# Expert weights taken in chunks of 1024 columns instead of 512, the last down product split by column half

## The chip, the cores and the metric

The kernel runs on one core of one Trainium2 chip. The metric is the device time of one execution in microseconds (us), as the median of several executions. The traces are of one profiled execution each.

## The reference

Two streams (256 prompt tokens and 64 sample tokens, 320 in all, width 1024) go through two layers. The second layer ends in a mixture of experts, which is what the change touches:

```
logits = (xf @ router).astype(jnp.float32)
top_v, top_i = lax.top_k(logits, TOP_K)                  # 2 of 8
gates = jax.nn.softmax(top_v, axis=-1)
for e in range(N_EXPERTS):
    y = y + combine[:, e:e + 1] * _swiglu(xf, w_gate[e], w_up[e], w_down[e])
# _swiglu: (silu(x @ w_gate) * (x @ w_up)) @ w_down, w_gate and w_up 1024 x 3584, w_down 3584 x 1024
x = layer_norm(ALPHA * x + y)
```

Everything is float32. All 8 experts' weights are read once (352 MB in the expert part).

## The kernel before

Every weight matrix comes in "units" of 1 MB (128 partitions x 2048 numbers). A unit passes four engines. SyncE issues its DMA into the ring `raw` (6 slots). ScalarE rounds it to the product format (`round_unit`, L993, writes `whi`). VectorE takes the remainder (`rest_unit`, L1250, writes `wlo = raw - whi`). TensorE multiplies with both: each float32 product is three products (hi*hi, hi*lo, lo*hi). `whi` and `wlo` are rings of 3 slots (SPLIT), so rounding unit n+3 waits until TensorE has used unit n, and both engines work two units ahead (AHEAD). Slots are in strict order: whatever stands between two units on ScalarE or VectorE delays the next unit.

Experts go in pairs, four pairs in this run: one `pair()` written out for the first, a loop for two, and one written out for the last (`FINAL`). For each pair 128 tokens per expert are gathered to `xg` (steps X, L877). A pair has 14 chunks of 512 columns (7 per expert), a chunk six units: gate (2 units, result in a PSUM bank), up (2 units, another bank), down (2 units, PSUM banks 4 and 5). The order is a list made by `pair_steps`: gate, T of the chunk before, gate, up, up, down of the chunk before twice. T turns the hidden rows: TensorE transposes `hm` (L931), ScalarE reads the bank into `hT_hi` (L1215), VectorE into `hT_lo` (L1764). After the second gate unit ScalarE makes `sg = silu(gate)` (L1191); after the second up unit VectorE makes `hm = sg * up` (L1738). Gate and up use banks 0 and 1 in even chunks, 2 and 3 in odd ones.

Small work hangs on VectorE behind `hm` of certain chunks: tables of the routing in the first pair (`tables`, chunks 0 to 7), the next pair's selection matrix (`make_pick`, L1672, chunk 9), and in the last pair the addresses of the tokens' rows (`rows_of_tokens`) and the sums of expert outputs into `acc` (`combine`, L1723: two each in chunks 6, 7 and 8, one in chunk 10, two in 11). In the last three chunks ScalarE and VectorE also split `acc` into `acc_hi` (L1197) and `acc_lo` (L1756). In the last chunk ScalarE loads the function table of the final norm (L1193).

Behind the last down product the residual `acc` is added through TensorE by an identity (`kept`, L951, L952), the last expert's output by the gate matrix (`newest`, L958 to L960), and VectorE normalizes three token tiles (L1788 to L1804).

Before the first pair, in `router()`, ScalarE and VectorE prepare x; the first two units are ready by then, the third is rounded only by `pair()`.

## Time and profile before

| | before |
|---|---|
| median of 3 executions | 1661.7 us (1661.43 to 1662.46) |
| the profiled execution | 1663.22 us, span of its instructions 1661.6 us |
| TensorE busy | 1630.2 us, 98% of the span |
| VectorE busy / ScalarE busy | 1228.0 us (74%) / 982.5 us (59%) |
| mean granted TensorE clock | 0.991 of full speed |
| expert part | from 638.64 us to the end |

The busy shares are over the whole span, of which the expert part is 62%. Idle time of an engine that is not the bottleneck costs nothing. The span and the execution's own time differ by 1.6 us, which no instruction of the trace fills.

### The profile page before, as it was taken

The page shows a single profiled execution, that of the slowest core. Times are in us where ns is not written, and L with a number is a line of the kernel's source. Part 1 is how long each engine was busy: PE and PEld are TensorE (multiplying, and loading weights), DVE is VectorE, ACT ScalarE, POOL GpSimd, SP SyncE. Part 2 cuts the span into 40 slices and gives each one's busy share as a digit, 9 for nine tenths or more (in the row PEclk, how much of TensorE's full clock was granted, in tenths as well). Part 3 has the DMA queues.
Part 4 walks back from the last instruction along what each step waited for, and adds up shares of the span by engine and source line. Part 5 has one row for each costly group of instructions (what it writes and reads, how often), then busy time and mean ns, then how long its engine had stood idle before and what let it go on. Part 6 is the DMA issues. An engine that isn't in the chain of part 4 may idle for free.

```text
span 1661.6 us, 22901 instructions
## 1 busy us (share of the span) xinstructions
PE 1630.2 (98%) x8756; PEld 1413.9 (85%) x8756; DVE 1228.0 (74%) x1050; ACT 982.5 (59%) x820; POOL 82.9 (5%) x91
## 2 busy tenths in 40 slices
PE   8999999999999999999999999999999999999996
PEld 7999999999989998787888888888888888777775
DVE  4567545445454766989887888887888888989987
ACT  4453433333344536777776777776777776776663
POOL 1001111111010000000000000000000000120200
PEclk8999999999999999999999999999999999999999
DMA  9424444444444243999998999998999999999992
GB/s 297 133 97 134 152 151 146 145 145 146 150 153 153 77 134 132 354 365 362 373 376 314 363 371 364 378 363 321 369 375 368 365 364 349 354 382 377 372 352 77
DMA packets 226500, 446.58 MB, mean 269 GB/s; under 512 B 10514, under 2 KB 72640, under 8 KB 226368
## 3 DMA queue, kind: packets, MB, share of 16 engines
q1 hardware_dynamic: 223856, 434.13, 73.5%
q0 software_dynamic: 2560, 11.29, 1.8%
q8 instruction: 58, 0.95, 0.2%
q14 instruction: 26, 0.21, 0.0%
HBM read 439.87 MB, written 8.67 MB: 270 GB/s over the span
## 4 chain that ended last, share of the span: by engine, by line
PE 88%; DVE 6%; ACT 2%; issue 2%; DMA 1%; SPq 1%; DVEq 0%; ACTq 0%
PE ps L918 15%; PE ps L901 12%; PE ps L903 12%; PE ps L902 12%; PE ps L590 10%; PE ps L592 10%; PE ps L591 10%; DVE wlo L1250 2%; ACT whi L993 2%; PE ps L877 1%; PE ps L931 1%; DMA raw<-in_moe_w_up 1%; PE ps L663 1%; PE ps L622 1%; DVE xl L1285 1%
## 5 line engine op out<-in xcount | busy, mean ns | idle before, releaser
L1250 DVE TENSOR_TENSOR wlo<-raw,whi 128x2048 fp32r<-128x2048 f32 x410 | 934.5, 2291 | 255.3 <-ACT whi L993 252.6
L993 ACT ACTIVATE whi<-raw 128x2048 fp32r<-128x2048 f32 x410 | 784.5, 1915 | 244.5 <-PE ps L592 85.1
L901 PE MATMUL ps<-whi,xg 128*128 128x512 f32 x896 | 360.9, 403 | 10.5 <-DVE wlo L1250 10.2
L903 PE MATMUL ps<-whi,xg 128*128 128x512 f32 x896 | 355.1, 396 | 0.0
L902 PE MATMUL ps<-wlo,xg 128*128 128x512 f32 x896 | 354.8, 396 | 0.0
L590 PE MATMUL ps<-xh,whi 128*128 128x320 f32 x832 | 259.8, 312 | 0.3
L591 PE MATMUL ps<-xl,whi 128*128 128x320 f32 x832 | 256.9, 309 | 0.0
L592 PE MATMUL ps<-xh,wlo 128*128 128x320 f32 x832 | 256.8, 309 | 0.0
L901 PEld LDWEIGHTS ps<-whi,xg 128*128 128x128 f32 x896 | 169.3, 189 | 55.4 <-DVE wlo L1250 15.5
L903 PEld LDWEIGHTS ps<-whi,xg 128*128 128x128 f32 x896 | 169.2, 189 | 40.1
L902 PEld LDWEIGHTS ps<-wlo,xg 128*128 128x128 f32 x896 | 169.4, 189 | 36.9
L590 PEld LDWEIGHTS ps<-xh,whi 128*128 128x128 f32 x832 | 156.5, 188 | 5.2 <-DVE xl L1285 2.4
L591 PEld LDWEIGHTS ps<-xl,whi 128*128 128x128 f32 x832 | 156.5, 188 | 0.2
L592 PEld LDWEIGHTS ps<-xh,wlo 128*128 128x128 f32 x832 | 156.4, 188 | 0.0
L918 PE MATMUL ps<-whi,hT_hi 128*128 128x512 f32 x448 | 140.8, 395 | 1.3 <-DVE wlo L1250 0.7
L918 PE MATMUL ps<-whi,hT_lo 128*128 128x512 f32 x448 | 141.0, 396 | 0.0
L918 PE MATMUL ps<-wlo,hT_hi 128*128 128x512 f32 x448 | 140.5, 394 | 0.0
L918 PEld LDWEIGHTS ps<-whi,hT_hi 128*128 128x128 f32 x448 | 83.9, 188 | 21.8 <-DVE wlo L1250 2.1
L918 PEld LDWEIGHTS ps<-whi,hT_lo 128*128 128x128 f32 x448 | 84.3, 188 | 19.9
L918 PEld LDWEIGHTS ps<-wlo,hT_hi 128*128 128x128 f32 x448 | 84.2, 188 | 19.9
L1215 ACT ACTIVATE hT_hi<-ps 128x512 fp32r<-128x512 f32 x56 | 33.6, 600 | 75.1 <-PE ps L931 74.8
L590 PE MATMUL ps<-hh,whi 128*128 128x320 f32 x224 | 69.0, 308 | 0.0
(287 smaller groups left out, 1378.8 us busy)
## 6 DMA issues: line engine op xcount, KB each, us to landing
raw<-in_moe_w_gate SPq DMA_DIRECT2D x112, 1024.0 KB, 7.4
raw<-in_moe_w_up SPq DMA_DIRECT2D x112, 1024.0 KB, 7.4
raw<-in_moe_w_down SPq DMA_DIRECT2D x112, 1024.0 KB, 6.9
raw<-in_w_in SPq DMA_DIRECT2D x24, 1024.0 KB, 5.5
raw<-in_ffn_w_gate SPq DMA_DIRECT2D x14, 1024.0 KB, 5.0
raw<-in_ffn_w_up SPq DMA_DIRECT2D x14, 1024.0 KB, 5.0
raw<-in_ffn_w_down SPq DMA_DIRECT2D x14, 1024.0 KB, 5.0
raw<-in_w_out SPq DMA_DIRECT2D x8, 1024.0 KB, 5.2
```

The lines of the kernel that those rows point to most:

```text
L590: pe.matmul(out, wh, hi, start=start and j == 0, stop=False)
L591: pe.matmul(out, wh, lo, start=False, stop=False)
L592: mm = pe.matmul(out, wl, hi, start=False, stop=stop and j == len(pairs) - 1)
L622: pe.matmul(bank[:, 0:P], mean_d[:], mean_d[:], start=True, stop=True)
L663: pe.matmul(ps[5][:, 0:T], mean_d[:], sq[:, k % 4, :], start=k == 0, stop=k == KT - 1).then_inc(var_part, 1)
L901: pe.matmul(bank[:], xh_k, wh, start=k == 0, stop=False)
L902: pe.matmul(bank[:], xh_k, wl, start=False, stop=False)
L903: mm = pe.matmul(bank[:], xl_k, wh, start=False, stop=k == KT - 1)
L918: mm = pe.matmul(ps[4 + d][:], hT[:, c % 2, k, :], slot(w, n, SPLIT, 2)[:, j, 512 * d:512 * d + 512], start=fc == 0 and k == 0 and hT is h ...
L993: act.activation(flat(whi, n, SPLIT), flat(raw, n, RAW), ACT.Copy).then_inc(hi_ready, 1)
L1215: act.activation(hT_hi[:, c % 2, :, :].rearrange("p f s -> p (f s)"), bank[:], ACT.Copy).then_inc(hT_hi_ready, 1)
L1250: dve.tensor_tensor(flat(wlo, n, SPLIT), flat(raw, n, RAW), flat(whi, n, SPLIT).bitcast(F32), ALU.subtract).then_inc(lo_ready, 1)
```

## The change

A chunk of a pair is now 1024 columns ("wide", number s, seven of them), except the middle one (s = 3, MID), which holds the last 512 columns of the first expert and the first 512 of the second. A gate or up unit of a wide chunk is 256 rows by 1024 columns (rows of 4 KB in memory instead of 2 KB), so gate fills banks 0 and 1, up banks 2 and 3, and there is no second set of banks. The number of units, products, transposes and bytes stays. Down units were rows of 4 KB already. A chunk is 4 gate units, T twice, 4 up units, 4 down units of the chunk before. Work that hung on chunk number c hangs on group g = 2s + q // 2 at up units with q = 1 or 3.

```diff
+        for s in range(WIDE):
+            steps += [("gate", s, q) for q in range(4)]
+            if s:
+                steps += [("T", s - 1, 0), ("T", s - 1, 1)]
+            if last and s == MID:
                 steps.append(("GT", 0, 0))
...
+            up = [("up", s, q) for q in range(4)]
+            down = [("down", s - 1, q) for q in range(4)] if s else []
+            if s == MID + 1:
+                steps += up[:2] + down[:2] + up[2:] + down[2:]
+            elif last and s == WIDE - 1:
+                steps += up + down[:2] + [("T", s, 0)] + down[2:] + [("T", s, 1)]
+            else:
+                steps += up + down
...
         if not last:
...
+            steps += [("X", 0, 0), ("X", 1, 0), ("T", WIDE - 1, 0), ("T", WIDE - 1, 1), ("X", 2, 0), ("X", 3, 0)]
+        return steps + [("down", WIDE - 1, q) for q in range(4)]
```

On ScalarE both silus stand behind the fourth gate unit, and the rounding of the third unit is moved from the start of `pair()` into `router()`, ahead of its reads of x (VectorE the same):

```diff
+                round_unit(U_MOE + AHEAD)
                 for n, j in enumerate(XT_ORDER):
...
-                        if part == "gate" and half:
+                        if part == "gate" and q == 3:
                             act.wait_ge(unit_used, upto(n + 1, i, PER_PAIR))
...
+                            if c:
+                                act.wait_ge(m_hid, upto(2 * c, i, PC))
+                            for b in range(2):
+                                act.activation(sg[:, b, :], ps[b][:], ACT.Silu).then_inc(m_silu, 1)
...
+                            if last and c == WIDE - 1:
                                 act.preload_act_table_set(LOG_EXP)
```

On VectorE:

```diff
-                        if part == "up" and half:
+                        if part == "up" and q == 3:
                             dve.wait_ge(unit_used, upto(n + 1, i, PER_PAIR))
...
+                            for b in range(2):
+                                dve.wait_ge(m_silu, upto(2 * c + b + 1, i, PC))
+                                dve.tensor_tensor(hm[:, b, :], sg[:, b, :], ps[2 + b][:], ALU.mult).then_inc(m_hid, 1)
+                        if part == "up" and q % 2:
+                            g = 2 * c + q // 2
                             if first:
...
+                                tables(g, step)
```

The last two down units of the last pair are multiplied together, first all for column half 0, then the residual of token tile 2, then all for half 1; the residuals of tiles 0 and 1 stand ahead of the last down product, and `combine` goes by column half:

```diff
+            def last_down(i, n):
...
+                pe.wait_ge(lo_ready, upto(n + 2, i, PER_PAIR))
+                for d in range(2):
+                    if d:
+                        kept(2)
+                    for q in (2, 3):
+                        for j in range(2):
+                            for hT, ws in ((hT_hi, (whi, wlo)), (hT_lo, (whi,))):
+                                for w in ws:
+                                    mm = pe.matmul(ps[4 + d][:], hT[:, 2 * q + j, :],
+                                                   slot(w, n + q - 2, SPLIT, 2)[:, j, 512 * d:512 * d + 512],
+                                                   start=False, stop=q == 3 and j == 1 and hT is hT_lo)
+                    mm.then_inc(ys_done, 1)
...
+            def combine():
...
+                for d, cols in enumerate(HALVES):
+                    pe.wait_ge(ys_lo_ready, d + 1)
+                    for t in range(TT):
```

VectorE's norm takes the statistics of column half 0 of all three tiles first, then goes tile by tile as before.

Where this moves instructions, in the order in which they stand on the engine. First ScalarE in the last chunk of the last pair, before, from the T ahead of the last gate unit:

```order
L1215 ACTIVATE hT_hi<-ps 128x512 [waits job_done]
L992 REGISTER_ALU [waits raw_landed3]
L993 ACTIVATE whi<-raw 128x2048 [waits unit_used]
L1189 REGISTER_ALU
L1190 REGISTER_ALU [waits unit_used]
L1191 ACTIVATE sg<-ps 128x512 [waits m_hid]
L1193 ACT_TABLE_LOAD
L993 ACTIVATE whi<-raw 128x2048 [waits unit_used,raw_landed4]
```

And ScalarE at the same place after the change (in the other wide chunks the rows are the same without the table load):

```order
L1030 ACTIVATE whi<-raw 128x2048 [waits unit_used]
L1227 REGISTER_ALU
L1229 REGISTER_ALU [waits unit_used]
L1231 ACTIVATE sg<-ps 128x512 [waits m_hid]
L1231 ACTIVATE sg<-ps 128x512
L1233 ACT_TABLE_LOAD
L1254 REGISTER_ALU
L1256 ACTIVATE hT_hi<-ps 128x512 [waits job_done]
L1254 REGISTER_ALU
L1256 ACTIVATE hT_hi<-ps 128x512 [waits job_done]
L1030 ACTIVATE whi<-raw 128x2048 [waits unit_used,raw_landed4]
```

Between two roundings stood one small operation at a time (one read of T, or one silu); now all four stand together. VectorE in the last pair, before, at chunk 7:

```order
L1250 TENSOR_TENSOR wlo<-raw,whi 128x2048 [waits hi_ready]
L1737 REGISTER_ALU [waits unit_used]
L1738 TENSOR_TENSOR hm<-sg,ps 128x512 [waits m_silu]
L1723 SCALAR_TENSOR_TENSOR acc<-y,gate_at,acc 128x1024 [waits y_fetched0]
L1723 SCALAR_TENSOR_TENSOR acc<-y,gate_at,acc 128x1024 [waits combined,y_fetched1]
L1249 REGISTER_ALU
L1250 TENSOR_TENSOR wlo<-raw,whi 128x2048 [waits hi_ready]
```

VectorE after the change, at groups 6 and 7 (s = 3):

```order
L1291 TENSOR_TENSOR wlo<-raw,whi 128x2048 [waits hi_ready]
L1765 SCALAR_TENSOR_TENSOR acc<-y,gate_at,acc 128x1024 [waits y_fetched0]
L1765 SCALAR_TENSOR_TENSOR acc<-y,gate_at,acc 128x1024 [waits combined,y_fetched1]
L1290 REGISTER_ALU
L1291 TENSOR_TENSOR wlo<-raw,whi 128x2048 [waits hi_ready]
L1290 REGISTER_ALU
L1291 TENSOR_TENSOR wlo<-raw,whi 128x2048 [waits hi_ready]
L1780 REGISTER_ALU [waits unit_used]
L1781 TENSOR_TENSOR hm<-sg,ps 128x512 [waits m_silu]
L1780 REGISTER_ALU
L1781 TENSOR_TENSOR hm<-sg,ps 128x512 [waits m_silu]
L1765 SCALAR_TENSOR_TENSOR acc<-y,gate_at,acc 128x1024 [waits y_fetched0]
```

The group at q = 1 has lost its `hm` product, the group at q = 3 has two of them ahead of its extra work.

## Rows read from the trace of the kernel before

**Rows 1.** The page's DMA issues: count, KB each, median us to landing.

```profile
raw<-in_moe_w_gate SPq DMA_DIRECT2D x112, 1024.0 KB, 7.4
raw<-in_moe_w_down SPq DMA_DIRECT2D x112, 1024.0 KB, 6.9
```

**Rows 2.** Waits, 640 to 1600 us: who waited for whom, us, times, longest.

```profile
ACT whi L993 <- DMA raw<-in_moe_w_gate: 5.1, 3, 2.8
PEld ps L901 <- issue: 3.0, 6, 0.7
```

**Rows 3.** The chain that ended last, inside the third pair: start us, us, what.

```profile
1163.81 5.58 PE ps L918 x24
...
1172.18 0.44 PE ps L931 x4
...
1180.98 5.57 PE ps L918 x24
```

**Rows 4.** Timeline in the second pair, around a silu: start us, us, engine, line.

```profile
909.82 0.40 PE L901 MATMUL ps<-whi,xg 128*128 128x512 f32 x1
...
910.02 0.60 ACT L1191 ACTIVATE sg<-ps 128x512 f32<-128x512 f32 x1 [0.39 <-PE ps L903]
...
910.52 1.91 ACT L993 ACTIVATE whi<-raw 128x2048 fp32r<-128x2048 f32 x1
...
912.46 4.61 DVE L1250 TENSOR_TENSOR wlo<-raw,whi 128x2048 fp32r<-128x2048 f32 x2 [0.51 <-ACT whi L993]
```

**Rows 5.** Timeline, the first product of the first expert pair.

```profile
638.64 0.39 PE L901 MATMUL ps<-whi,xg 128*128 128x512 f32 x1
```

**Rows 6.** The chain that ended last, first pair, around its third unit.

```profile
642.53 1.82 ACT whi L993
...
646.72 0.50 PE ps L901
...
648.05 0.43 PE ps L902
```

**Rows 7.** Windows: busy us (count) of each engine, PEclk, DMA share, GB/s.

```profile
647.80:651.00 3.20, 3.20 (x9) 2.51 (x8) 3.20 (x2) 0.61 (x1) 0.00 (x0) 0.50 0.89 308
...
1600.00:1603.40 3.40, 3.40 (x10) 2.52 (x10) 3.14 (x2) 0.00 (x0) 0.00 (x0) 0.51 0.95 327
```

**Rows 8.** Timeline in the router: both engines' idle time before.

```profile
622.98 0.56 DVE L1570 COPY lg<-ps 128x8 f32<-128x8 f32 x3 [5.25 <-PE ps L839]
...
623.96 0.60 ACT L1158 ACTIVATE xt_hi<-ps 128x512 fp32r<-128x512 f32 x1 [5.66 <-PE ps L848]
```

**Rows 9.** Timeline of VectorE, last pair, chunks 6 and 7.

```profile
1501.32 0.68 DVE L1738 TENSOR_TENSOR hm<-sg,ps 128x512 f32<-128x512 f32 x1
1501.91 2.67 DVE L1723 SCALAR_TENSOR_TENSOR acc<-y,gate_at,acc 128x1024 f32<-128x1024 f32 x2
...
1504.50 6.69 DVE L1250 TENSOR_TENSOR wlo<-raw,whi 128x2048 fp32r<-128x2048 f32 x3
...
1520.12 0.68 DVE L1738 TENSOR_TENSOR hm<-sg,ps 128x512 f32<-128x512 f32 x1
```

**Rows 10.** Timeline of VectorE, second pair, chunk 9.

```profile
1055.45 0.95 DVE L1672 TENSOR_TENSOR pick<-slot_no,q_tab 128x768 fp32r<-128x768 f32 x1
```

**Rows 11.** Timeline of TensorE, last pair, behind chunk 11.

```profile
1598.79 0.51 PE L901 MATMUL ps<-whi,xg 128*128 128x512 f32 x1 [2.29 <-DVE wlo L1250]
```

**Rows 12.** Timeline of the end.

```profile
1624.70 1.28 ACT L1193 ACT_TABLE_LOAD   x1
...
1630.29 0.73 PE L918 MATMUL ps<-whi,hT_hi 128*128 128x512 f32 x2 [0.74 <-DVE wlo L1250]
...
1637.11 0.73 PE L918 MATMUL ps<-whi,hT_hi 128*128 128x512 f32 x2 [0.54 <-DVE hT_lo L1764]
...
1642.79 0.39 PE L951 MATMUL ps<-acc_hi,ident_r 128*128 128x512 f32 x1
...
1645.55 1.31 DVE L1788 BATCH_NORM_STATS2 stats<-ps 128x6 f32<-128x512 f32 x2 [0.65 <-PE ps L960]
```

More of the change, by code:

```diff
@@ L883, in pair @@
                 unit, job = 0, GATHERS
-                for part, c, half in steps:
-                    a, fc = c // FC, c % FC
-                    if first and (part, c, half) == ("gate", 1, 0):
-                        pe.wait_ge(acc_ready, 2 * TT)
+                for part, c, q in steps:
+                    a = expert_of(c, q)
                     if part in ("gate", "up"):
@@ L1728, in pair @@
                 unit, job, turns = 0, GATHERS, 0
-                for part, c, half in steps:
+                for part, c, q in steps:
                     if part in ("gate", "up", "down"):
```

229 lines of the change are left out of this document (116 added, 113 removed).

## The prediction

> **What bounds the kernel now.** I read the page first, for the busy shares and the DMA issues, then the waits of the expert part, then the chain that ended last, then the timeline around each place that the change touches. TensorE is 98% busy, and in the expert part it is the bound in a plain sense: in the third pair one chunk takes 17.17 us from down product to down product, of which the 24 products of down are 5.57, a T is 0.44, and the 48 products of gate and up are the 11.16 left [rows 3]. So a product takes 0.232 us, whether its weights came in rows of 2 KB (gate, up) or of 4 KB (down), and a unit of 12 takes 2.79. There is no idle time in such a chunk to win. DMA is no bound: a 2 KB-row unit lands 7.4 us after its issue and a 4 KB-row unit 6.9 [rows 1], and the longest wait of a rounding for a gate transfer is 2.8 us, three waits and 5.1 us in all [rows 2].
>
> TensorE waits elsewhere. At the start of the experts the third unit is late: the first product starts at 638.64 [rows 5], two units later it is 644.22, the third unit starts at 646.72 because ScalarE rounds it only at 642.53 [rows 6]. And in the first and last pair VectorE's small work makes units late. These waits and the end are where the change can act.
>
> **The margin behind each unit.** Take as zero the moment at which a unit's next product starts. ScalarE's silu starts at +0.20 (910.02 against 909.82), the rounding behind it 0.50 later, VectorE's remainder 1.95 after the start of the rounding [rows 4]. A remainder takes 2.29 alone. TensorE continues about 0.17 after its end (from the case below). So before, +0.20 +0.50 +1.95 +2.29 +0.17 = 5.1, against 5.58 for the two units in hand: 0.47 to spare. On VectorE the same: at chunk 6 of the last pair hm starts at 1501.32, the sums follow at 1501.91, the next remainder only at 1504.50, and the next hm is 18.80 later than this one instead of 17.17 [rows 9]. So 0.59 for hm and 2.59 of extra work x cost 1.63: stall = x + 0.6 for each hm product - 1.56.
>
> **Part by part.**
>
> *Third unit rounded in the router: -4.1.* It removes the wait of 2.5 us (644.22 to 646.72). Behind it products stood at 0.43 instead of 0.23 [rows 6], the granted clock being 0.50, that is 1.2 GHz in place of 2.4 [rows 7]; eight such products lost 1.6. The cover in the router: ScalarE was idle for 5.66 us and VectorE for 5.25 [rows 8]; rounding 1.9 and remainder 2.3 in line are 4.2, so they fit with some 0.4 to 1 to spare; without that cover up to 4.2 would stand in front of the reads of x. The fourth unit is now the one rounded at 642.53; 642.53 + 1.95 + 2.29 + 0.17 = 646.94, and it is wanted at 647.01. What is late next: nothing.
>
> *Silus and T reads together: +2.3.* Behind the fourth gate unit ScalarE now has two silus and two reads of T before the next rounding: 0.20 + 4 x 0.50 + 1.95 + 2.29 + 0.17 = 6.6. TensorE has two T's and two units: 0.88 + 5.58 = 6.46. The wait is 0.1 to 0.15 each, in six chunks of four pairs, of which the last is taken below: 23 x 0.1 = 2.3. The margin is thinner than what I can read, so between 0 and 0.25 each: 0 to 5.8. Queued behind ScalarE's silus are only these roundings, and VectorE's remainder and TensorE wait for them in turn. With no T in the way (s = 0) two silus need 5.6 against 5.58: nothing.
>
> *Two hm products together: nothing in a plain chunk* (1.2 - 1.56 < 0), but in a group with extra work the even ones gain 0.6 and the odd ones lose 0.6, each cut off at zero. First pair, tables: before, six waits and 3.0 in all [rows 2], of which 2.2 show in the distances of the chunks. Groups 1, 5, 7 lose 0.6 each, groups 2 and 6 give back 0.15 and 0.6, group 3 (0.4) and the selection matrix in group 9 (0.65) begin to show: **+2.1**. Second and third pair: the matrix is 0.95 [rows 10], 0.87 to the next start; it was hidden (0.87 + 0.6 < 1.56), now 0.87 + 1.2 - 1.56 = 0.5 twice: **+1.0**. Last pair: groups 6 and 8 gain 0.6 each, group 7 loses 0.6 (1.6 to 2.2), group 11 loses 0.6 (TensorE's idle of 2.29 [rows 11], counted by distance 2.56, becomes 3.2), groups 0, 2 and 10 gain 0.1, 0.4 and 0.2, groups 1 and 3 lose 0.6 and 0.1: **0**.
>
> *Gathers: +0.5.* T twice between X1 and X2 lets X2 wait for the bank of the first T: 0.2 more, three times (an estimate; the T operations' 0.6 and 0.7 on ScalarE and VectorE follow each other, TensorE's T is 0.44).
>
> *The end: +3.6.* (a) The table load of 1.28 [rows 12] stood between one silu and a rounding and made the first down product of chunk 12 late by 0.9 (idle 0.74 [rows 12]). Now it stands in the row of four operations that has no margin: 0.1 + 1.3 = 1.5 at least. (b) In the last chunk hm twice and a split of acc (1.13 from start to start) give 0.77, less T's 0.44, plus 0.35 since (a) leaves VectorE later: 0.7; before 0.15. (c) `last_down` wants both last units at once. The last one reuses the slot of down unit 80 (counted in the pair), so its rounding starts only when 80 is used: 0.20 + 1.95 + 2.29 + 0.17 = 4.6 after it, while TensorE has just unit 81 in hand (2.79): 1.8. Before, the last but one product waited 0.8 for hT_lo (idle 0.54 [rows 12]), which goes. (a) to (c): 4.0 against 1.85, +2.1. (d) Twelve residual products of 0.2275, 2.7 us, stood behind the last down product at 1642.79 and now stand ahead of its end, where nothing idles long enough to hide them; in return the statistics begin 1.5 after that end (second column half to ys_lo 0.8, then 0.6) instead of 2.8 (1645.55). VectorE's tail is as long as before. +2.7 - 1.3 = +1.4.
>
> *4 KB rows: 0.* The transfers hide behind 11 us of units in the ring; of the waits in rows 2 at most 1.2 reached TensorE. The Trainium skill (DMA: Bandwidth & Descriptors, Where 436 GB/s comes from) puts the limit of a core's loads from HBM at about 358 GB/s, whatever the rows. By that rule longer rows would bring nothing either; the trace does not agree with the figure, since a unit of 1.049 MB in 2.79 us is 376 GB/s.
>
> **Sum**: -4.1 + 2.3 + 2.1 + 1.0 + 0 + 0.5 + 3.6 = +5.4. The profiled execution took 1663.2 and would take 1668.6; the median of the runs shown is 1.5 below it, so 1661.7 + 5.4 = **1667.1**.
>
> **Rivals.**
> - *The clock falls again.* Idle times of 2.5 and 2.6 us were followed by 3.4 us at 1.2 GHz [rows 7], those of 1.6 were not. The 2.2 of group 7 and the 1.5 and 1.8 of the end lie between. Each fall costs 1.6: one or two give 1668.7 to 1670.3. Chance 0.20. The Trainium skill (TensorE: Matmul & The Clock Gate, What's actually happening) says that activity releases the throttle and lack of it brings it back; the trace agrees.
> - *ScalarE's queue has just enough margin.* With no wait behind the silus 1667.1 - 2.3, and with the gathers' 0.5 hidden too 1664.3, within what counts as no change. Against it stands only a difference of 0.1. Chance 0.20.
> - *The product itself gets faster* (the other side). 4 KB rows might ease what slows a product; 2% off the 2688 gate and up products is 12.5 us, 1654.6. It decides from 8.7 us, 3.2 ns a product. For it: products step by 0.2275 at the very end, with no weights arriving. Against it: down products, with 4 KB rows, take the same 0.232 as gate and up [rows 3]. Chance 0.12.
> - *The silu wait is 0.25 or more* and adds up with late transfers: 1670 to 1672. Chance 0.06. The forecast itself has the 0.42 left.
>
> **How the numbers follow.** 0.2% (3.3 us) is what a measurement of this kernel can tell from no change. Faster: the third rival, 0.12. Same, up to 1665.0: the second rival and a lower part of the forecast, 0.24. Slower: 0.64. The range takes in the clock above and part of the faster case below: 1659.0 to 1671.5; the forecast's own is 1664.5 to 1670.
>
> **What would show it.** In the changed kernel the third unit should start 5.58 after the first, with the granted clock at 1.0. A chunk of the middle pairs should take 34.4 to 34.5 instead of 2 x 17.17 = 34.34; the chain should name ScalarE's hT_hi and a rounding at the first up unit. Group 9 should show 0.5 of idle, group 11 some 3.2 with slow products behind it. In the end, 1.8 of idle ahead of `last_down` on the remainder of the last unit, and statistics 1.5 behind the last product. A middle chunk under 34.2 would make me wrong as a whole; so would a product step under 0.230.

## The result: 1678.1 us against 1662.0, slower by 1.0%

The changed kernel takes 1678.08 us (median of 4 runs, 1677.68 to 1681.39) against 1661.99 for the kernel before beside it (4 runs, 1661.43 to 1662.46). The ratio is 1.0103, 95% interval 1.0088 to 1.0118. The prediction had 1667.1 and a range up to 1671.5: the direction was right, the loss of 16.1 us three times the 5.4 predicted. The profiled execution is the slowest of its four, 1681.39 us.

The loss by stretch, from the profiled spans of 1661.6 and 1679.8. The experts start at the same time (638.6). Between first gate loads the three pairs take 253.64, 251.49 and 249.79 us, where they took 253.84, 248.26 and 247.38; the last pair up to the end of TensorE's last product takes 273.1 instead of 261.8, and the tail behind that 13.1 instead of 11.8. So of the 18.2 us between the spans 11.4 are in the last pair.

The page of the changed kernel, DMA packets and DMA issues:

```profile
DMA packets 177347, 446.57 MB, mean 266 GB/s; under 512 B 10514, under 2 KB 72640, under 8 KB 177216
...
raw<-in_moe_w_gate SPq DMA_DIRECT2D x112, 1024.0 KB, 7.0
raw<-in_moe_w_up SPq DMA_DIRECT2D x112, 1024.0 KB, 7.3
raw<-in_moe_w_down SPq DMA_DIRECT2D x112, 1024.0 KB, 7.3
```

A gate unit now lands in 7.0 us instead of 7.4 [rows 1], a down unit, whose rows have not changed, in 7.3 instead of 6.9. The longer rows bought no time on the path.

**The start.** Timeline of the router in the changed kernel, then the first pair around the third unit:

```profile
618.80 1.89 ACT L1030 ACTIVATE whi<-raw 128x2048 fp32r<-128x2048 f32 x1
620.79 2.29 DVE L1291 TENSOR_TENSOR wlo<-raw,whi 128x2048 fp32r<-128x2048 f32 x1 [2.46 <-ACT whi L1030]
623.00 0.55 DVE L1612 COPY lg<-ps 128x8 f32<-128x8 f32 x3
623.81 0.60 ACT L1196 ACTIVATE xt_hi<-ps 128x512 fp32r<-128x512 f32 x1 [3.12 <-PE ps L862]
...
638.67 0.39 PE L921 MATMUL ps<-whi,xg 128*128 128x512 f32 x1
...
644.25 0.40 PE L921 MATMUL ps<-whi,xg 128*128 128x512 f32 x1
644.48 0.39 PE L922 MATMUL ps<-wlo,xg 128*128 128x512 f32 x1
```

Rounding and remainder fit into the idle time of [rows 8] (the copy of lg starts at 623.00 instead of 622.98), and the third unit starts at 644.25, 5.58 behind the first, where TensorE waited until 646.72 [rows 6].

**The last pair.** Who waited for whom on TensorE's weight loads, 1390 to 1640 us, in the changed kernel:

```profile
PEld ps L921 <- DVE wlo L1291: 9.7, 10, 2.7
PEld ps L947 <- DVE wlo L1291: 9.5, 9, 3.7
PEld ps L965 <- DVE hT_lo L1808: 1.8, 1, 1.8
```

The rows add up to 21 us, where the kernel before had 14.4 (L901 12.3 and L918 2.1). Almost all is VectorE's remainder being late, but not always because of VectorE. The longest wait of the first row, 2.66, goes back over a rounding to a weight transfer. Timeline around it, and the DMA issues of the same 30 us (1445 to 1475):

```profile
1463.91 1.92 ACT L1030 ACTIVATE whi<-raw 128x2048 fp32r<-128x2048 f32 x1 [2.83 <-DMA raw<-in_moe_w_up]
...
1473.49 0.50 PE L921 MATMUL ps<-whi,xg 128*128 128x512 f32 x1 [2.22 <-DVE wlo L1291]
...
raw<-in_moe_w_up SPq DMA_DIRECT2D x4, 1024.0 KB, 15.3
y<-y_park,row_i POOLq DMA_INDIRECT x6, 10.4
```

While the gathers of the tokens' rows are in flight a unit lands 15.3 us after its issue; between 1400 and 1430 it was 6.4. The kernel before has the same gathers, and two waits of 0.52 and 0.79 on its weight loads there. In the other runs a wait there is anything from nothing to 3.05 us. No run moves the gathers, so that they cause the late landings is not shown.

VectorE's timeline around groups 6 and 7, and TensorE's idle time behind both, then behind groups 8 and 11, and at the turn of the combine matrix (GT, L965):

```profile
1504.17 0.64 PE L965 MATMUL ps<-ident,x 128*128 128x128 f32 x3 [1.60 <-DVE hT_lo L1808]
...
1513.41 2.67 DVE L1765 SCALAR_TENSOR_TENSOR acc<-y,gate_at,acc 128x1024 f32<-128x1024 f32 x2
1515.99 4.49 DVE L1291 TENSOR_TENSOR wlo<-raw,whi 128x2048 fp32r<-128x2048 f32 x2
...
1518.34 0.74 PE L947 MATMUL ps<-whi,hT_hi 128*128 128x512 f32 x2 [0.64 <-DVE wlo L1291]
1520.40 1.28 DVE L1781 TENSOR_TENSOR hm<-sg,ps 128x512 f32<-128x512 f32 x2
1521.59 2.67 DVE L1765 SCALAR_TENSOR_TENSOR acc<-y,gate_at,acc 128x1024 f32<-128x1024 f32 x2
1524.18 4.48 DVE L1291 TENSOR_TENSOR wlo<-raw,whi 128x2048 fp32r<-128x2048 f32 x2
1526.52 1.22 PE L947 MATMUL ps<-whi,hT_hi 128*128 128x512 f32 x2 [2.33 <-DVE wlo L1291]
...
1558.36 0.50 PE L921 MATMUL ps<-whi,xg 128*128 128x512 f32 x1 [1.12 <-DVE wlo L1291]
...
1602.02 1.22 PE L947 MATMUL ps<-whi,hT_hi 128*128 128x512 f32 x2 [3.27 <-DVE wlo L1291]
```

Read the starts on VectorE. The sums of group 6 start at 1513.41, those of group 7 only 8.2 us later, at 1521.59; between them stand two remainders and two hm products with no idle time. In [rows 9] one chunk of 18.8 us lay between one such piece and the next. Group 11 waits 3.27 where [rows 11] has 2.29. (Idle times in the rows of PE are those between products. On the weight loads, PEld, the same waits are 0.2 to 0.45 longer: 2.76 behind group 7 and 3.71 behind group 11.)

The granted clock in windows behind these waits (the columns are those of [rows 7]; PEclk is the third number from the end):

```profile
1506.00:1509.40 3.40, 3.40 (x9) 2.64 (x8) 2.28 (x1) 1.24 (x2) 0.00 (x0) 0.50 1.02 407
1526.50:1529.90 3.40, 3.38 (x8) 2.71 (x9) 3.40 (x2) 0.00 (x0) 0.00 (x0) 0.51 0.69 210
1601.90:1604.50 2.60, 2.48 (x6) 2.00 (x7) 2.60 (x3) 0.00 (x0) 0.00 (x0) 0.50 0.56 142
```

Three stretches at 1.2 GHz in the last pair, where before there was one.

**The loop's back edge and the end.** TensorE's timeline where the third pair starts, which is where its loop jumps back, and then the end:

```profile
1143.69 0.50 PE L921 MATMUL ps<-whi,xg 128*128 128x512 f32 x1 [1.04 <-issue]
...
1621.62 1.28 ACT L1233 ACT_TABLE_LOAD   x1
1628.18 0.50 PE L921 MATMUL ps<-whi,xg 128*128 128x512 f32 x1 [1.32 <-DVE wlo L1291]
1655.70 0.51 PE L993 MATMUL ps<-whi,hT_hi 128*128 128x512 f32 x1 [1.53 <-DVE wlo L1291]
1663.76 2.47 DVE L1836 BATCH_NORM_STATS2 stats<-ps 128x6 f32<-128x512 f32 x4
```

The first row is a wait that no part of the prediction has. The others are the table load's 1.3 instead of 0.74 [rows 12], the wait for both last units, and the statistics, which start 1.3 behind the end of the last down product (1662.48) where 1.5 was predicted.

### The profile page after: what moved, and what is told of

Its sections match the earlier page's. It is cut to its first block, busy times and chain, and to the rows that moved or that the text cites. A ratio compares the mean times of both kernels' runs of the same rounds, so it can differ in the third digit from the quotient of the medians.

```text
span 1679.8 us, 22854 instructions
## 1 busy us (share of the span) xinstructions
PE 1634.3 (97%) x8756; PEld 1414.7 (84%) x8756; DVE 1228.8 (73%) x1050; ACT 980.1 (58%) x820; POOL 81.7 (5%) x91
## 4 chain that ended last, share of the span: by engine, by line
PE 80%; DVE 11%; ACT 4%; issue 4%; DMA 1%; SPq 1%; DVEq 0%; ACTq 0%
PE ps L947 14%; PE ps L604 10%; PE ps L606 10%; PE ps L605 10%; PE ps L921 10%; PE ps L923 9%; PE ps L922 9%; DVE wlo L1291 6%; ACT whi L1030 2%; PE ps L891 1%; DMA raw<-in_moe_w_up 1%; PE ps L960 1%; DVE hm L1781 1%; ACT hT_hi L1256 1%; PE ps L677 1%
## 5 line engine op out<-in xcount | busy, mean ns | idle before, releaser
L921 PEld LDWEIGHTS ps<-whi,xg 128*128 128x128 f32 x896 | 169.3, 189 | 58.5 <-DVE wlo L1291 18.8
L947 PEld LDWEIGHTS ps<-whi,hT_hi 128*128 128x128 f32 x440 | 82.1, 191 | 33.4 <-DVE wlo L1291 11.3
L606 PE MATMUL ps<-hh,wlo 128*128 128x320 f32 x224 | 69.5, 310 | 0.0
```

Source lines behind the costliest of these rows:

```text
L606: mm = pe.matmul(out, wl, hi, start=False, stop=stop and j == len(pairs) - 1)
L921: pe.matmul(bank[:], xh_k, wh, start=k == 0, stop=False)
L947: mm = pe.matmul(ps[4 + d][:], hT[:, 2 * q + j, :], slot(w, n, SPLIT, 2)[:, j, 512 * d:512 * d + 512], start=opens and j == 0 and hT is hT ...
```

## Experiments

Sixteen kernels, each with a profile and 4 to 11 timed runs beside the kernel before on the same chip, whose medians were 1661.7 to 1662.7 us. An interval is some 0.13% (2 us) to either side.

| run | us | ratio to before, 95% |
| --- | --- | --- |
| t_apart | 1673.59 | 1.0062 (1.0049 to 1.0076) |
| gt_earlier | 1677.02 | 1.0089 (1.0074 to 1.0104) |
| end_as_before | 1675.37 | 1.0086 (1.0072 to 1.0100) |
| rows_of_2k | 1677.65 | 1.0095 (1.0080 to 1.0111) |
| before_third_unit | 1659.78 | 0.9978 (0.9968 to 0.9988) |
| before_end_by_half | 1663.74 | 1.0006 (0.9997 to 1.0015) |
| before_spread | 1645.07 | 0.9894 (0.9879 to 0.9909) |
| wide_apart_spread | 1656.86 | 0.9960 (0.9946 to 0.9973) |
| wide_silu_hm_apart | 1655.59 | 0.9962 (0.9949 to 0.9974) |
| wide_x_late | 1655.67 | 0.9962 (0.9950 to 0.9975) |
| wide_all | 1649.42 | 0.9923 (0.9910 to 0.9936) |
| before_spread_x | 1642.29 | 0.9884 (0.9869 to 0.9898) |
| after_spread | 1664.77 | 1.0019 (1.0008 to 1.0029) |
| wide_all_x_late | 1650.75 | 0.9937 (0.9924 to 0.9951) |
| odd_work_later | 1670.77 | 1.0050 (1.0037 to 1.0063) |
| even_work_earlier | 1690.76 | 1.0157 (1.0143 to 1.0170) |

### Single parts of the change undone

**t_apart**: on the changed kernel,

```diff
-            steps += [("gate", s, q) for q in range(4)]
-            if s:
-                steps += [("T", s - 1, 0), ("T", s - 1, 1)]
+            for q in range(4):
+                steps.append(("gate", s, q))
+                if s and q < 2:
+                    steps.append(("T", s - 1, q))
```

> The changed kernel, but the two T products of a chunk of 1024 columns no longer stand together behind the fourth gate unit: the first stands behind gate unit 0, the second behind gate unit 1 of the next chunk. Theory (the ScalarE queue of two silus and two reads of T ahead of a rounding is what costs): the stall of about 0.2 us at each of 23 turns goes (-4.5), in the last pair T no longer stands directly ahead of the gate table's turn (wait of 1.8 us at 1504.17, -1.9) and the clock fall behind it goes (-1.5): 6 to 8 us below the changed kernel. A wide chunk without extra work should take 34.35 instead of 34.55 us. Rival (these stalls are VectorE's or the transfers', and the place of T only moves them): within 1 us of the changed kernel, chunks still 34.55.

1673.59, 4.1 us below rows_of_2k, which ran beside it and stands for the changed kernel, and 4.5 below the changed kernel's own median. The chunks do what was said. TensorE's timeline, second pair, changed kernel: the first down product of three chunks.

```profile
938.42 0.64 PE L947 MATMUL ps<-whi,hT_hi 128*128 128x512 f32 x2
...
972.94 0.62 PE L947 MATMUL ps<-whi,hT_hi 128*128 128x512 f32 x2
...
1007.45 0.63 PE L947 MATMUL ps<-whi,hT_hi 128*128 128x512 f32 x2
```

34.52 and 34.51 us; with T apart the same rows stand at 936.10 and 970.55, 34.45. Before, two chunks of the third pair took 2 x 17.17 = 34.34. But 17.17 is not the same everywhere. TensorE's timeline of the kernel before, second pair, the down products two chunks apart:

```profile
949.89 0.63 PE L918 MATMUL ps<-whi,hT_hi 128*128 128x512 f32 x2
...
984.36 0.63 PE L918 MATMUL ps<-whi,hT_hi 128*128 128x512 f32 x2
```

That is 34.47, or 17.23 a chunk, in all twelve chunks of that pair; in before_third_unit it is the third pair that has 17.23. So the T in a row cost 0.05 to 0.17 a chunk, depending on the pair.

The pairs took 252.13, 250.74 and 249.13, so 1.5, 0.7 and 0.7 less. In the second and third that is no more than the turns of 0.1 that were predicted. In the first a wait of 1.26 on the weight loads behind group 1 is gone as well, and in the last pair the same wait falls from 1.62 to 0.55: TensorE now has both T, 0.44 each, to do ahead of that unit. The rest comes from the last pair too. 6 to 8 was too much, since the idle time behind group 6 grew from 0.64 to 0.91 once TensorE was no longer held up at GT, and the profile still has three falls of the clock. The one behind GT is gone as the theory says, but another one stands behind a wait for a late transfer (3.05 on the weight loads at 1469).

**gt_earlier**: on the changed kernel,

```diff
-            steps += [("gate", s, q) for q in range(4)]
+            for q in range(4):
+                steps.append(("gate", s, q))
+                if last and s == MID and q == 1:
+                    steps.append(("GT", 0, 0))
```

> The changed kernel, but the turn of the combine matrix (GT) in the last pair stands behind the second gate unit of the middle chunk and not right behind the two T. Theory (three turns in a row over two banks, each of which waits for ScalarE and VectorE, made the idle time of 1.8 us, and that idle time made the clock fall behind it): 1.8 to 3.4 us below the changed kernel, no granted clock of 0.5 near 1506. Rival (the wait belongs to the late DMA episode at 1468 and the units are late anyway): within 0.5 us.

1677.02, 0.6 below rows_of_2k and 1.1 below the changed kernel's own median, which is inside the interval: less than the theory's lower bound. The wait at GT is gone, but the next one grows. Timeline of gt_earlier, GT and the first down unit behind group 6:

```profile
1494.16 0.58 PE L966 MATMUL ps<-ident,x 128*128 128x128 f32 x3
...
1513.87 0.73 PE L948 MATMUL ps<-whi,hT_hi 128*128 128x512 f32 x2 [1.13 <-DVE wlo L1292]
```

1.13 in place of 0.64: TensorE had been held up by 1.6 at GT, which had given VectorE time to catch up. A wait that lets the late engine catch up is not worth its length. This profile has no fall of the clock near 1506, but neither has that of rows_of_2k with its GT where it was, so it does not say what moving GT does for the clock.

**end_as_before**: the list of the last chunk, `combine` and the statistics as in the kernel before,

```diff
-                        if steps is FINAL and (c, q) == (WIDE - 1, 0):
-                            pe.wait_ge(m_hid, upto(PC, i, PC))
-                            kept(0)
-                            kept(1)
-                        if steps is FINAL and c == WIDE - 1 and q in (2, 3):
-                            if q == 2:
-                                last_down(i, n)
-                            continue
...
+                kept(0)
+                kept(1)
+                newest(0)
+                newest(1)
+                kept(2)
+                newest(2)
```

> The changed kernel with the end of the kernel before: last down product by unit, residual products behind it, statistics in the old order. Theory of the prediction: the wait of 1.7 us for both last units goes, the residual products go back behind the end (+2.7 and -1.3 of the prediction reversed): 3 us below the changed kernel. Rival (residual products ahead of the end cost nothing, since TensorE waits there anyway for the roundings): 0 to 0.5 below, or above it by up to 1.3.

1675.37: 2.7 below the changed kernel's median, 2.3 below rows_of_2k. The expected 3 is inside the interval, but so is the rival's 0 to 0.5. The profiles speak for the theory: against rows_of_2k, with one fall of the clock in the last pair each, the last pair is 2.4 shorter (266.3 against 268.7) and the tail 1.3 (11.8 against 13.15).

**before_end_by_half** puts that end on the kernel before (the diff is the one of the change, `last_down` with `half` in place of `q`).

> The kernel before with the end of the change alone: residual products of the first two tiles ahead of the last down product, the last two down units as one product by column half, combination and statistics by column half. Prediction's own terms: wait for both last units about +1.0 more than before, residual products ahead and earlier statistics +1.4: together +1 to +2.4. Rival (the residual products ahead of the end fill TensorE's wait for the last unit): -1.3 to 0.

1663.74, 1.1 above the kernel before beside it, at the lower end of the term; the interval of the ratio goes from 0.5 below to 2.5 above, so it doesn't exclude the rival's 0. With small chunks the wait ahead of `last_down` is 0.5 us of weight-load idle time, not 2.0.

**rows_of_2k**: two transfers of 512 columns for each wide gate and up unit,

```diff
+                    for h in range(2):
+                        src = w[0, bass.ds(e, 1), row:row + P * n, f + 512 * h:f + 512 * h + 512].rearrange(
+                            "e (k p) d -> p (e k) d", p=P)
+                        sp.dma_start(slot(raw, m, RAW, n)[:, :, 512 * h:512 * h + 512], src
+                                     ).then_inc(raw_landed[m % RAW], 16)
```

> The changed kernel, but each gate and up unit of a 1024-column chunk is loaded by two transfers of 512 columns each, so with rows of 2 KB as before the change. Theory (rows of 4 KB bring nothing, transfers hide behind the ring): within 0.8 us of the changed kernel, the product step stays at 0.2325 us. Rival (longer rows help the transfers and with them the margins at the ends of the ring): 2 us or more above the changed kernel, with more waits of ScalarE for transfers.

1677.65 against 1678.08, with 229584 packets instead of 177347. The rows of 4 KB are worth nothing here, as predicted.

**before_third_unit**: `round_unit(U_MOE + AHEAD)` and `rest_unit(U_MOE + AHEAD)` in the router of the kernel before, and not in its first pair.

> The kernel before with one part of the change alone: the third expert unit is rounded in the router, ahead of the reads of x. Theory of the prediction: 2.5 us of wait and 1.6 us of slow clock go, so 4.1 us below the kernel before. Rival (the wait only moves to the fourth unit, or the roundings in the router push the reads of x): 0 to 1.5 below.

1659.78: 2.9 us by the medians, 3.7 by the ratio (2.0 to 5.3). The profiled first pair is 249.79 instead of 253.84, which is the predicted 4.1. That the medians gain less has a likely reason, which before_end_by_half shows. Windows of that kernel, whose first pair is the same as in the kernel before:

```profile
647.80:651.00 3.20, 3.20 (x15) 2.59 (x15) 3.16 (x2) 1.75 (x2) 0.00 (x0) 1.00 0.82 306
1600.00:1603.40 3.40, 3.40 (x18) 2.81 (x17) 3.40 (x2) 0.70 (x2) 0.00 (x0) 1.00 0.97 304
```

Its third unit waited 2.33 us, as long as before, and the clock stayed at 2.4 GHz, where [rows 7] have 0.50. So the 1.6 us of slow clock is there in some executions only.

### Where VectorE's small work stands

**before_spread**: on the kernel before, the third unit in the router, the table load behind the last rounding, and a second place for small work in each chunk,

```diff
+                        if part == "down" and half and c < PC - 1:
                             if first:
+                                tables(c + 1, step)
+                            if not last and c + 1 == 9:
                                 make_pick(1 if first else dve.snap(i + 1))
+                            if last:
+                                rows_of_tokens(c + 1, step)
+                                if 6 <= c + 1 < 6 + TT:
+                                    combine(1, y_2, c + 1 - 6)
```

> The kernel before (chunks of 512) with the third unit in the router, the table load behind the last rounding, and VectorE's small work (tables, sums, matrix, split of acc) given a second place in each chunk, at the second down unit of the chunk before. Theory (VectorE's and ScalarE's extra work in one place of the ring is what stalls the first and the last pair, not the width of the chunks): about 12 us below the kernel before: -4.1 third unit, -2 tables, -5 sums and falls of the clock behind them, -0.9 table load. Rival (the stalls come from transfers and the clock whatever the place of the work): only the -4.1 of the third unit.

1645.07: 17.6 us below the kernel before, where the theory had 12, and 14.7 below before_third_unit. Of these 14.7 the profiles show 2.6 in the first pair and 11.6 in the last, where one fall of the clock is gone too. TensorE's waits in the last pair, 1380 to 1640 us:

```profile
PEld ps L901 <- DVE wlo L1251: 2.5, 8, 0.4
PEld ps L918 <- DVE wlo L1251: 0.4, 1, 0.4
```

14.4 us have become 2.9. The sums stand one at a time, as VectorE's timeline of this kernel shows:

```profile
1492.52 1.28 DVE L1725 SCALAR_TENSOR_TENSOR acc<-y,gate_at,acc 128x1024 f32<-128x1024 f32 x1
1493.71 4.49 DVE L1251 TENSOR_TENSOR wlo<-raw,whi 128x2048 fp32r<-128x2048 f32 x2
1498.12 1.28 DVE L1725 SCALAR_TENSOR_TENSOR acc<-y,gate_at,acc 128x1024 f32<-128x1024 f32 x1
```

One piece of 1.19 (1492.52 to 1493.71) behind one hm product costs 1.19 + 0.6 - 1.56 = 0.2 by the prediction's rule, and 0.36 to 0.42 are seen on the weight loads, of which part costs nothing; two in a row cost 1.6.

**after_spread** and **wide_apart_spread** are the changed kernel with the same spreading, the T together and apart.

> The changed kernel with the table load behind the last rounding and VectorE's small work spread, but with the two T still together. Without the wide chunks the same two edits took 14.7 us (1659.8 to 1645.1); with T apart 16.7 (1673.6 to 1656.9). Theory (pairs of hm products make the small work dearer only by the 2 us between these, and the T in a row cost 4.5 by themselves): 1661 to 1662. Rival (most of the loss is the interplay of T in a row with the small work, so it goes with either edit): 1658 or less.

> The changed kernel with the two T apart, the table load behind the last rounding, and VectorE's small work spread over up and down units. Theory (1024 columns cost nothing by themselves, only the bunching of reads and of small work): within 2 us of the same edits on chunks of 512 plus the changed end's +1 to +2, so about 11 us below the kernel before and 26 below the changed kernel. Rival (the wide chunk has a cost of its own: pairs of hm, silu and T reads leave less margin everywhere): 5 us or more above the version with chunks of 512.

1664.77 and 1656.86. So the T in a row cost 7.9 us once the small work is out of the way, not 4.5: the pairs differ by 1.4, 0.6 and 0.5, the last one by 5.3 (262.42 against 257.16), of which a wait at GT of 1.83 on the weight loads and a fall of the clock behind it are part. (By the ratios, each to its own neighbours, it is 9.8.) Neither theory of after_spread had that; the two costs do not add, which fits that each hides part of the other. And wide_apart_spread still takes 11.8 us more than before_spread. The changed end, the pairs of silus and hm products and the wait at the loop's edge are in that too; it alone doesn't tell what the width costs. The section on the wide chunk takes them out.

**odd_work_later** and **even_work_earlier** leave each piece whole and only move it, on the changed kernel:

```diff
-                        if part == "up" and q % 2:
-                            g = 2 * c + q // 2
+    def work_at(part, c, q):
+        if part == "up" and (q == 1 or (q == 3 and c in (0, WIDE - 1))):
+            return 2 * c + q // 2
+        if part == "down" and c < WIDE - 2 and q == (2 if c == MID else 1):
+            return 2 * (c + 1) + 1
```

this is odd_work_later (the `g` of a step is what `work_at` returns, on ScalarE's split of acc too), and in even_work_earlier the function is

```diff
+    def work_at(part, c, q):
+        if (part, q) == ("gate", 0):
+            return 2 * c
+        return 2 * c + 1 if (part, q) == ("up", 3) else None
```

> The changed kernel, but VectorE's small work of the odd groups 3 to 11 stands behind the second down unit that follows, four or more units behind that of the even group instead of two, and no longer directly behind the two hm products. No piece is split. Theory (two pieces of small work two units apart are what VectorE can't take, since it gains some 0.5 us per unit; the second piece finds it late): idle time of group 7 falls from 2.8 to 1.0 to 1.3 us, that of group 11 from 3.7 to 2.2 or less, group 9's 0.9 go; with fewer falls of the clock 6 to 9 us below the changed kernel. Rival (the stall is set by the piece alone, wherever it stands): group 11 still above 3, at most 2 us below.

> The changed kernel, but the small work of the even groups stands at the first gate unit, six units ahead of that of the odd group, which stays directly behind the two hm products. Theory (distance between the pieces): group 7 and 11 fall to what the prediction's rule gives for two hm products in front of a piece, 2.2 and 3.1 us (seen 2.8 and 3.7), even groups 1.0 to 1.6 as before; but the even pieces are now late at the two silus and the two T: between 3 below and 2 above the changed kernel. Rival (only the two hm products in front of the odd piece count): 2.8 and 3.7 stay.

odd_work_later: 1670.77, 7.3 us below the changed kernel and 6.9 below rows_of_2k, inside the theory's 6 to 9. Its pairs are 250.28, 251.34 and 249.09, the last one 266.6. TensorE's timeline behind groups 7 and 11:

```profile
1523.41 0.51 PE L928 MATMUL ps<-whi,xg 128*128 128x512 f32 x1 [1.16 <-DVE wlo L1299]
...
1596.22 0.50 PE L928 MATMUL ps<-whi,xg 128*128 128x512 f32 x1 [2.08 <-DVE wlo L1299]
```

2.33 has become 1.16, 3.27 has become 2.08 (on the weight loads 2.76 has become 1.58 and 3.71 has become 2.51, somewhat more than the 1.3 and 2.2 of the theory). Both waits fell by 1.2, which is the length of the two hm products that no longer stand in front. So this run alone doesn't tell distance from hm products, and its 7.3 us are not the cost of the distance. even_work_earlier does tell them apart, since the hm products stay in front of the odd piece there and only the even piece moves away. TensorE's timeline behind groups 7 and 11 in even_work_earlier:

```profile
1526.31 0.72 PE L952 MATMUL ps<-whi,hT_hi 128*128 128x512 f32 x2 [1.92 <-DVE wlo L1297]
...
1613.80 0.73 PE L952 MATMUL ps<-whi,hT_hi 128*128 128x512 f32 x2 [2.89 <-DVE wlo L1297]
```

2.33 has become 1.92, 3.27 has become 2.89. By distance the same waits are some 0.28 longer (before, 1.35 is 1.63 and 2.29 is 2.56), so 2.2 and 3.2: what the prediction's rule gives for two hm products in front of a piece. The distance between two pieces is worth 0.4 us each here, the rest is the pair of hm. The kernel as a whole is slower, 1690.76, for a reason that was not foreseen. Waits of VectorE, 1570 to 1592 us:

```profile
DVE acc L1771 <- DMA y<-y_park,row_i: 11.4, 1, 11.4
```

Group 10's sum now asks for rows that the gather has not brought yet, TensorE stands still for 11.3 us and the clock falls with it.

### What the wide chunk still costs

**wide_silu_hm_apart**: on wide_apart_spread, ScalarE's second silu behind the next rounding, VectorE's second hm behind the next remainder,

```diff
+                            act.activation(sg[:, 0, :], ps[0][:], ACT.Silu).then_inc(m_silu, 1)
+                        if (part, q) == ("up", 0):
+                            act.activation(sg[:, 1, :], ps[1][:], ACT.Silu).then_inc(m_silu, 1)
```

> The version of wide chunks with T apart and the small work spread, and now the two silus of a chunk stand on both sides of a rounding, and the two hm products on both sides of a remainder. Theory (what the wide chunk still costs is that silus and hm products come in pairs ahead of one unit): the 0.22 us of PEld idle time at the second gate unit of each chunk goes (about 0.12 each, 23 times: 2.8), and part of the stalls of the last pair: 3 to 6 us below that version. Rival (the idle time belongs to the first T read or to late transfers): within 1 us of it.

1655.59, 1.3 below by the medians and nothing by the ratios: the rival. Most of the idle times of 0.22 do go, yet the chunks keep their 34.41 to 34.47 us, so such short idle times on the weight loads were no loss. What makes the wide chunk 0.12 longer than 34.34 stays open; the kernel before has the same 34.47 in its second pair, so the width need not be the reason.

**wide_x_late** moves X2 and X3, **wide_all** has every repair and spreads the gathers, **wide_all_x_late** is wide_all with the gathers of wide_x_late:

```diff
-            steps += [("X", 0, 0), ("X", 1, 0), ("T", WIDE - 1, 0), ("T", WIDE - 1, 1), ("X", 2, 0), ("X", 3, 0)]
+            steps += [("X", 0, 0), ("X", 1, 0), ("T", WIDE - 1, 0), ("T", WIDE - 1, 1)]
+            steps += [("down", WIDE - 1, 0), ("down", WIDE - 1, 1), ("X", 2, 0), ("X", 3, 0)]
+            return steps + [("down", WIDE - 1, 2), ("down", WIDE - 1, 3)]
```

> The version of wide chunks with T apart and the small work spread, and now X2 and X3 stand between the second and the third of the last four down units, so that two down units follow the last gather as in the kernel before. Theory (the idle time of 1.95 us at the loop's back edge, put down to issue or to wlo, comes from TensorE's sequencer reaching the end of the loop's body late, because the wait for the last down unit holds it): unchanged, since the last down unit is still the last thing in the body and the wait for it stays: idle time of 1.5 to 2 us at the edge. Rival (the gathers' reads, bunched ahead of four down units, make the units behind the edge late): the idle time at the edge falls under 0.3 and the time by 1.4 to 1.7 us.

> Wide chunks with every repair: third unit in the router, T apart, silus and hm products apart, small work spread, gathers spread between the down units, the end of the kernel before, table load behind the last rounding. Theory (the width of 1024 columns costs nothing once nothing is bunched): within 2 us of the version with chunks of 512 and spread small work, about 1645 to 1648. Rival (an unavoidable cost of the wide chunk remains, in the last pair above all): 1650 or more.

> The version of wide chunks with every repair, but the gathers placed as in the version where two of them stand between the second and the third of the last four down units, since that one showed 0.65 us of idle time at the loop's back edge and the one with spread gathers 3.11 and a slow clock behind it. Theory (the place of the gathers sets the idle time at the edge): 0.5 to 0.8 us there, the waits of 1.0 us for the first gather's read come back three times (+1 to +2), so within 1 us of 1649.4. Rival (the idle time at the edge depends on something else, such as where the code lies or how busy the transfers are): 1.5 us or more at the edge.

1655.67, 1649.42 and 1650.75. The idle time at the back edge was 1.95 us on the weight loads in wide_apart_spread, 0.65 in wide_x_late and 0.75 in wide_all_x_late, but 3.11 in wide_all. TensorE's timeline of wide_all at the edge, and the DMA queues of the same kernel from 1132.3 to 1132.6, where its last product ahead of the edge ends:

```profile
1135.06 0.50 PE L924 MATMUL ps<-whi,xg 128*128 128x512 f32 x1 [2.67 <-issue]
...
q8 instruction: 1, 0.02, 19.7%
```

So the place of the gathers changes it, as wide_all_x_late was to show, but by a rule that neither theory of wide_x_late had: two down units behind the last gather give 0.65 in one order and 3.11 in another. The timeline names no releaser (in two kernels VectorE's remainder), but the DMA queues show what happens at this place. In the last row above (queue, packets, MB, share of the 16 engines) one packet of 16 KB passes in the queue "instruction", which by its name brings program code. There is one in some 27 us, and in each of the 18 profiles an additional one starts ahead of this edge, the only place where the loop jumps back. In wide_all it starts at 1132.41 and the next product 2.65 us later; in the changed kernel at 1141.01, and the product at 1143.69, 2.68 later. In 13 of the 14 kernels with 0.65 us of idle time or more on the weight loads this distance is 2.63 to 2.73 (the 14th, odd_work_later, has 2.90, with a packet that took 1.34 us instead of some 0.95); in the four with 0.24 or none it is 2.94 to 3.04. So the idle time is what is left of some 2.65 us when TensorE's work ahead of the edge runs out: in wide_all that work ends as the packet starts, in the kernel before it goes on behind it. The Trainium skill (Runtime: NRT & Kernel Launch, Instruction fetch mechanics) says that a taken branch outside what has been fetched has to wait for a fetch by DMA; the traces agree. What makes TensorE's sequencer reach the jump earlier or later is not shown.

wide_all is 4.3 above before_spread, more than its theory's 2, and no wide version came within 4 us of it. The fetch and a late transfer, with a fall of the clock behind each, are in wide_all's profile. They are not the whole: wide_all_x_late has 0.75 at the edge, no fall and no wait for a late transfer, its end is the old one, and its pairs are still 1.3, 1.6, 1.1 and 1.9 us longer than those of before_spread. So the theory that the width costs nothing has no run behind it.

**before_spread_x**: on before_spread,

```diff
-            steps += [("X", 0, 0), ("X", 1, 0), ("T", PC - 1, 0), ("X", 2, 0), ("X", 3, 0)]
+            steps = steps[:-1] + [("X", 0, 0), ("T", PC - 1, 0)] + steps[-1:] + [("X", 1, 0), ("X", 2, 0)]
+            return steps + [("down", PC - 1, 0), ("X", 3, 0), ("down", PC - 1, 1)]
```

> The version with chunks of 512, third unit in the router and small work spread, and now the four gathers and the T between them are spread between the last three down units. Theory (T waits 1.0 us for VectorE's read of the first gather, three times, since four gathers and a T share two banks): the three waits go, 2.5 to 3.5 us below that version, about 1642. Rival (the reads, moved between roundings, make the down units late instead): no change or up to 2 us slower.

1642.29, the fastest of all, 20.2 below the kernel before beside it (ratio 0.9884, which is 1.7 us better than before_spread's). The three waits of 1.0 us for a gather's read are gone: the pairs take 245.97, 246.72 and 246.78.

## Why the prediction was right in direction and wrong in size

- *Third unit, -4.1*: right as a mechanism and in the profiled pair (-4.05); 2.9 by the medians and 3.7 by the ratio, and the fall of the clock behind the wait was seen not to come in every execution.
- *Silus and T reads, +2.3*: 0.05 to 0.17 a chunk in the middle pairs against the predicted 0.1, inside its bounds. The step failed in the last pair, where it was counted like any other: there the T in a row stand ahead of GT (idle 1.60). Undoing it gave 4.1 to 4.5 (a wait of group 1 in the first and the last pair is in that), and 7.9 where the small work was spread.
- *Two hm products together, +2.1, +1.0 and 0*: **this is the step that failed**, the prediction's "groups 6 and 8 gain 0.6 each, group 7 loses 0.6, group 11 loses 0.6 ... Last pair: 0". The rule for a single group was good: with the pieces seven and five units apart, in even_work_earlier, groups 7 and 11 wait the 2.2 and 3.2 that it gives. But it takes for granted that VectorE comes to each piece on time. In the changed kernel an even and an odd piece are two units apart instead of six, and ten units follow without one, which makes each of these two waits 0.4 longer still. On the weight loads groups 7 and 11 lost 1.0 each instead of 0.6 (1.79 to 2.76, 2.73 to 3.71), group 1 too (0.60 to 1.62), group 3 lost 0.7 instead of 0.1, and group 0 lost 0.5 where it was to gain 0.1; group 6 gained 0.7, group 8 only 0.2 of its 0.6. All in all some 2.6 in place of "Last pair: 0". In the first pair the same waits grew by 3.4 instead of 2.1, and the selection matrix in group 9 shows 1.0 to 1.1 instead of 0.5. Moving the odd pieces away gave back 7.3 us, but that also takes away the one hm product that stood in front of each of them before the change, so it can't be set against the step's 3.1.
- *Gathers, +0.5*: not separated. The 1.0 us wait for a gather's read was there before as well. What was missed is the back edge, 1.0 us between products and 1.5 on the weight loads.
- *The end, +3.6*: right as far as it can be told. Table load 1.32 of idle time against 1.5 predicted, `last_down` 1.53 against 1.8, the tail 1.3 longer against 1.4; undoing (b) to (d) gave 2.3 to 2.7, with an interval that has 0 in it.
- *4 KB rows, 0*: right (1677.65 against 1678.08). But "DMA is no bound" is not so in the last pair: there late landings made TensorE wait 2.9 us on the weight loads in this profile and 1.3 in the one before. The 376 GB/s of that step is a core's rate with no other core of the chip at work; no run here shows it beside a second one, so it is weak evidence against the figure quoted there.
- *The rival of the clock* was priced right (1.6 each) and given 0.20. Two falls more than before are in the profiled execution, and it is 3.3 us above the median. It goes with the other causes, it is no case of its own. rows_of_2k and end_as_before, with the same waits at these places, have one fall each in their profiles, so how many come is chance.
- *The product faster*: wrong, its step stayed at 0.232.

How much of the 10.7 us above the prediction belongs to what can be read from the profiled executions only, which differ by 18.2 us instead of 5.4. Against the prediction's own terms the first pair is 1.0 too long, the second 1.9, the third 1.1, and the last with the tail 8.6. In the second that is the back edge and the selection matrix. In the last it is two more falls of the clock (3.2 by the price of 1.6 each), the groups' waits (2.6), the wait at GT (1.8) and the late transfers (1.6 more than before). That is somewhat more than 8.6, since idle time on the weight loads is partly hidden. It is an account from two traces: no run takes these apart one by one.

## What to carry to other kernels

A margin per unit is not enough to cost a change; look at what now stands directly in front of each extra piece of work (0.6 us for each hm product here), and ask how many units lie between one piece and the next on the same engine, because the second one meets an engine that is still late (0.4 here). When steps are grouped into larger chunks, everything that hung on the old, smaller chunk is bunched with them: give each small piece a place of its own in the new order before judging the grouping, and check that a piece moved earlier doesn't get ahead of the transfer that it reads. Here the place of some small work and a table load, worth 14.7 us, mattered more than the row length and the chunk width that the change was about.

## What the runs showed that was not expected

- The same idle time is not always followed by the slow clock. Behind 2.33 us at 1526.52 the changed kernel had 0.51; rows_of_2k, with 2.32 at the same place, had this window:

```profile
1523.00:1526.40 3.40, 3.40 (x15) 2.76 (x16) 3.40 (x2) 0.33 (x1) 0.00 (x0) 1.00 0.67 192
```

  In the expert part of these traces idle times of 1.83 to 3.33 on the weight loads went either way, and none under 1.8 was followed by a fall; behind the 3.71 of group 11 it came all five times. The Trainium skill (TensorE: Matmul & The Clock Gate, What's actually happening) lets lack of activity bring the throttle back; the traces agree, but the length of one idle time does not tell whether it does.
- Idle times of 0.2 us on the weight loads, tens of them, cost nothing that the pair distances show, while the product behind starts on time.
- TensorE's idle time at a loop's back edge went from nothing to 3.1 us with the order of a few steps in the body, and the product behind it never started less than 2.63 us after the start of the instruction packet.
